# Softmax probabilities and values of a decoder's attention: from f32 to pairs of f16 halves

## What is computed

```python
def one_block(args):                       # 128 queries
    score = jnp.einsum('bqh,bqhs->bqs', iws, jax.nn.relu(dots))
    _, sel = lax.top_k(score, topk)        # 256 keys of each query
    kg, vg = gather_kv(sel)
    logits = jnp.einsum('bqgrd,bqkgd->bqgrk', qg, kg) * (HEAD_DIM ** -0.5)
    logits = jnp.where(valid, logits + bias, -jnp.inf)
    p = jax.nn.softmax(logits, axis=-1).astype(vg.dtype)
    o = jnp.einsum('bqgrk,bqkgd->bqgrd', p, vg)
```

## Time and profile before

| | |
|---|---|
| Median of 3 runs | 4112.12 us (4103.06 to 4114.4) |
| Profiled execution, its own time | 4099.31 us |
| Span of the profile | 4097.5 us |
| PE busy | 3281.3 us, 80% |
| DVE busy | 1911.3 us, 47% |
| ACT busy | 1566.2 us, 38% |
| POOL busy | 1078.0 us, 26% |
| Granted PE clock, mean | 0.90 |

### The profile page before, as it was taken

The page is one execution under the profiler, slowest core; times in us unless marked ns, Lnnn a source line. Parts: engine busy times, 40 slices in busy tenths (PEclk is TensorE's granted clock), DMA queues, the critical chain, the costliest instruction groups (busy, mean ns, idle before and its releaser), DMA issues.

```text
span 4097.5 us, 68214 instructions
## 1 busy us (share of the span) xinstructions
PE 3281.3 (80%) x26714; PEld 2622.8 (64%) x26714; DVE 1911.3 (47%) x3962; ACT 1566.2 (38%) x2674; POOL 1078.0 (26%) x979
## 2 busy tenths in 40 slices
PE   5958677288777897888798897889788897998597
PEld 3747555166455675677586785767667686676486
DVE  3635345634742235624474237732487324884100
ACT  2233332432632225432373226533265432754211
POOL 0131530022542114312341114311242112420142
PEclk9969888589889998899899999999999999999798
DMA  5426564045343453325252353414334043340254
GB/s 159 136 66 230 172 199 161 6 148 170 112 136 123 140 170 107 114 90 175 96 170 71 112 165 100 144 39 159 122 119 132 29 150 118 124 144 1 93 179 140
DMA packets 200579, 514.25 MB, mean 126 GB/s; under 512 B 20242, under 2 KB 79458, under 8 KB 200130
## 3 DMA queue, kind: packets, MB, share of 16 engines
q1 hardware_dynamic: 200258, 509.88, 38.1%
HBM read 443.67 MB, written 66.15 MB: 124 GB/s over the span
## 4 chain that ended last, share of the span: by engine, by line
issue 29%; PE 22%; ACT 8%; DVE 8%; POOLq 7%; POOL 4%; DMA 2%; ACTq 1%; DVEq 1%; SPq 0%
PE bank L784 4%; PE bank L785 4%; PE bank L786 4%; PE bank L833 4%; ACT T L1419 3%; DMA FR<-in_xT 2%; DVE T L1551 2%; POOLq L2016 1%; POOLq L2013 1%; POOLq L2011 1%; PE bank L822 1%; POOLq L1898 1%; POOL FR L2019 1%; ACTq L1421 1%; PE bank L809 1%
## 5 line engine op out<-in xcount | busy, mean ns | idle before, releaser
L784 PE MATMUL bank<-FR,ring 128*128 128x256 f16 (+1 forms) x4224 | 1189.3, 282 | 82.1 <-POOLq L580 23.7
L785 PE MATMUL bank<-FR,ring 128*128 128x256 f16 (+1 forms) x4224 | 1187.6, 281 | 0.0
L786 PE MATMUL bank<-FR,ring 128*128 128x256 f16 (+1 forms) x4224 | 1186.3, 281 | 0.0
L784 PEld LDWEIGHTS bank<-FR,ring 128*128 128x128 f16 x4224 | 423.0, 100 | 165.9 <-ACT ev L1360 27.4
L785 PEld LDWEIGHTS bank<-FR,ring 128*128 128x128 f16 x4224 | 420.6, 100 | 70.7 <-issue 1.1
L786 PEld LDWEIGHTS bank<-FR,ring 128*128 128x128 f16 x4224 | 420.3, 100 | 71.1
L784 PE MATMUL bank<-T,ring 128*128 128x256 f16 (+3 forms) x1280 | 370.2, 289 | 102.1 <-DVE kT L1661 52.4
L1551 DVE CUSTOM_DVE_ANT_0 T<-bank,T 128x256 f32<-128x256 f32 (+3 forms) x384 | 194.8, 534 | 531.8 <-PE bank L811 422.0
L833 PE MATMUL bank<-vtok,T 128*128 128x64 f32 x2176 | 321.2, 293 | 101.6 <-DVE T L1564 76.3
L833 PEld LDWEIGHTS bank<-vtok,T 128*128 128x128 f32 x2176 | 301.9, 213 | 126.8 <-issue 74.8
L785 PE MATMUL bank<-T,ring 128*128 128x256 f16 (+3 forms) x1280 | 369.1, 288 | 0.0
(11 more groups left out here) (305 smaller groups left out, 5970.4 us busy)
## 6 DMA issues: line engine op xcount, KB each, us to landing
ring<-halves_kept SPq DMA_DIRECT2D x605, 512.0 KB, 3.5
halves_kept<-ring SPq DMA_DIRECT2D x93, 512.0 KB, 5.2
ring<-halves_kept SPq DMA_DIRECT2D x52, 384.0 KB, 3.5
kT<-in_w_gu SPq DMA_DIRECT2D x33, 512.0 KB, 5.9
kT<-in_w_in SPq DMA_DIRECT2D x18, 512.0 KB, 5.9
ikT<-in_w_gu SPq DMA_DIRECT2D x17, 512.0 KB, 6.2
T<-in_xT SPq DMA_DIRECT2D x8, 1024.0 KB, 6.4
FR<-in_xT SPq DMA_DIRECT2D x8, 1024.0 KB, 10.0
```

The source lines that it names most:

```text
L784: mm(o, lhs[0], rhs[0], start=first, stop=False)
L785: mm(o, lhs[0], rhs[1], start=False, stop=False)
L786: return mm(o, lhs[1], rhs[0], start=False, stop=last)
```

## The change

Probabilities and values become pairs of f16 halves, scaled up by 1024 and 16 so that the low halves are not lost; `scale` divides by both. `values` is `three` f16 products (high x high, high x low, low x high) in place of one f32 product. ACT writes the high half of a group's probabilities (semaphore a_pTh); a new DVE instruction in `low_pT` reads the same bank again, multiplies and subtracts the high half, and only then counts a_pTc. DVE's order in step A of unit n is now: `mask` of n + 1, `low_pT` of group 0, `scale` of n - 2, `low_pT` of the other groups. The low half of the turned output is formed by DVE (`low_mix`) from PSUM, so that POOL's `mix_low`, ACT's second copy and the buffer mix32 go. The projection's values are written to an f32 buffer of their own (v32, for the output) and as the high half by ACT; DVE forms the low half. `PLAN` is the same.

```diff
-        vtok = sb("vtok", [128, SEQ // 128, 128])
+        vtok = sb("vtok", [128, SEQ // 128, 2, KVH * HD], F16)
+        v32 = sb("v32", [128, 2, KVH * HD])
-        pT = cut(T, 8192, 3, 4, 128)
+        pT = T[:, 8192:9728].bitcast(F16).rearrange("p (m s t n) -> p m s t n", s=2, t=4, n=128)
...
-                    last = mm(bank[6 + u % 2][:, 0:64], pT[:, GN[i, h, g] % 3, t % 4, :], vtok[:, t, e:e + 64],
-                              start=(t == 0), stop=(t == i))
+                    last = three(bank[6 + u % 2][:, 0:64], [pT[:, GN[i, h, g] % 3, s, t % 4, :] for s in range(2)],
+                                 [vtok[:, t, s, e:e + 64] for s in range(2)], t == 0, t == i)
...
-                A(pT[:, m % 3, 0:w, :], bank[4 + n % 2][:, 0:128 * w].rearrange("p (t n) -> p t n", n=128),
-                  ACT.Copy).then_inc(S("a_pTc"), 1)
+                A(pT[:, m % 3, 0, 0:w, :], bank[4 + n % 2][:, 0:128 * w].rearrange("p (t n) -> p t n", n=128),
+                  ACT.Copy, scale=P_UP).then_inc(S("a_pTh"), 1)
...
+                        A(v32[:, :, :], rows, ACT.Copy, scale=back)
+                        last = A(vtok[:, 2 * b:2 * b + 2, 0, :], rows, ACT.Copy, scale=V_UP * back)
...
+            def low_pT(i, h, g):
+                n, m = TN[i, h, g], GN[i, h, g]
+                dve.wait_ge(S("a_pTh"), n + 1)
+                w = min(4, i + 1 - 4 * g)
+                v.scalar_tensor_tensor(pT[:, m % 3, 1, 0:w, :],
+                                       bank[4 + n % 2][:, 0:128 * w].rearrange("p (t n) -> p t n", n=128), P_UP,
+                                       pT[:, m % 3, 0, 0:w, :], ALU.mult, ALU.subtract).then_inc(S("a_pTc"), 1)
+
+            def low_mix(i):
+                n = TN[i, "out", 0]
+                dve.wait_ge(S("a_pTh"), n + 1)
+                high, low = (mixA[:, s, :, 128 * (i % 2):128 * (i % 2) + 128] for s in range(2))
+                v.scalar_tensor_tensor(low, bank[4 + n % 2][:, :].rearrange("p (j n) -> p j n", n=128), M_UP, high,
+                                       ALU.mult, ALU.subtract).then_inc(S("a_pTc"), 1)
...
+                    if what == "v":
+                        wait_evacuated(dve, *step)
+                        v.scalar_tensor_tensor(vtok[:, 2 * b:2 * b + 2, 1, :], v32[:, :, :], V_UP,
+                                               vtok[:, 2 * b:2 * b + 2, 0, :], ALU.mult, ALU.subtract)
...
                 if kind == "A":
                     units = [(i, h) for i in tiles_of(b) for h in range(HEADS)]
                     n = step[2]
+                    i, h = units[n]
                     if n + 1 < UNITS:
                         mask(*units[n + 1])
+                    low_pT(i, h, 0)
                     if n >= 2:
                         scale(*units[n - 2])
+                    for g in range(1, groups(i)):
+                        low_pT(i, h, g)
+                    if n == HEADS + 1:
+                        low_mix(2 * b)
```

More of the change, by code:

```diff
@@ L56 @@
 I_UP = 16.0
+V_UP, P_UP = 16.0, 1024.0
 W_UP, H_UP, M_UP, U_UP = 256.0, 64.0, 16.0, 4.0
@@ L536, in layer @@
         relu = cut(T, 4096, 4, 512)
-        pT = cut(T, 8192, 3, 4, 128)
+        pT = T[:, 8192:9728].bitcast(F16).rearrange("p (m s t n) -> p m s t n", s=2, t=4, n=128)
         nearm = cut(T, 9728, 2, 256)
         osb = cut(T, 10240, 2, 512)
-        mix32 = cut(T, 11264, 4, 128)
         marks = T[:, 11776:12800].bitcast(F16)
@@ L562, in layer @@
         raw_room = [
-            vtok[:, 8:16, :].rearrange("p t n -> p (t n)").rearrange("p (a n) -> p a n", a=2),
+            vtok[:, 8:16, :, :].rearrange("p t s n -> p (t s n)").bitcast(F32).rearrange("p (a n) -> p a n", a=2),
             ikT[:, :, 1024:2048].bitcast(F32),
@@ L725, in _ @@
                     sp.dma_start(a["o_v"][t0:t0 + TOK].rearrange("(t p) n -> p t n", p=128),
-                                 vtok[:, 2 * b:2 * b + 2, :]).then_inc(S("outputs"), 16)
-                    outs += 16
+                                 v32[:, :, :]).then_inc(S("out_k"), 16)
                     if b == 0:
@@ L767, in _ @@
             sp.wait_ge(S("outputs"), outs)
-            sp.wait_ge(S("out_k"), 32 * NBLK)
+            sp.wait_ge(S("out_k"), 48 * NBLK)
             sp.wait_ge(S("out_gs"), 16)
@@ L1186, in copy_mix @@
                 act.wait_ge(S("a_pT"), n + 1)
[L1187 to L1191, removed]
+                A(mixA[:, 0, :, 128 * (i % 2):128 * (i % 2) + 128],
+                  bank[4 + n % 2][:, :].rearrange("p (j n) -> p j n", n=128), ACT.Copy, scale=M_UP
+                  ).then_inc(S("a_pTh"), 1)
             def sample_probs(s):
@@ L1251, in _ @@
                     if what == "v":
-                        last = A(vtok[:, 2 * b:2 * b + 2, :], o[:, 0:256].rearrange("p (t c) -> p t c", c=128), ACT.Copy,
-                                 scale=back)
+                        if b:
+                            act.wait_ge(S("out_k"), 48 * b)
+                        rows = o[:, 0:256].rearrange("p (t c) -> p t c", c=128)
+                        A(v32[:, :, :], rows, ACT.Copy, scale=back)
+                        last = A(vtok[:, 2 * b:2 * b + 2, 0, :], rows, ACT.Copy, scale=V_UP * back)
                         if b == 0:
@@ L1564, in scale @@
                 v.tensor_scalar(osb[:, i % 2, 64 * h:64 * h + 64], bank[6 + u % 2][:, 0:64],
-                                rden[:, u % 4:u % 4 + 1], None, ALU.mult).then_inc(S("a_scaled"), 1)
+                                rden[:, u % 4:u % 4 + 1], 1.0 / (P_UP * V_UP), ALU.mult, ALU.mult).then_inc(S("a_scaled"), 1)
             def biased(s):
@@ L1654, in _ @@
                             if b:
-                                dve.wait_ge(S("out_k"), 32 * b)
+                                dve.wait_ge(S("out_k"), 48 * b)
                             v.tensor_scalar(k32[:, j:j + nj, :], oj, back, None, ALU.mult)
@@ L1877, in _ @@
                     scale(2 * b + 1, HEADS - 1)
+                    low_mix(2 * b + 1)
         @block.gpsimd
@@ L1907, in near @@
                                 ).then_inc(S("a_near"), 1)
[L1909 to L1912, removed]
             for at, step in enumerate(PLAN):
@@ L2055, in _ @@
                         near(*units[n + 1])
[L2056 to L2059, removed]
 def outputs_of():
```

## The result

The changed kernel takes **4189.19 us** (median; 4186.02 to 4191.63), the kernel before 4113.26 us beside it (4103.06 to 4116.16): ratio 1.0186, 95% interval 1.0167 to 1.0205. It is 76 us slower. The spans of the two profiled executions differ by more, 4189.8 - 4097.5 = 92.3 us, because the one of before, at 4099.31 us, lies under all four of its timed runs and the one after, at 4191.63, is the slowest of its four. Differences between traces are held against 92.3 here, medians against 76.

A forecast was written before the change was run, and what follows sets the result against it. The bound was taken as a loop through three queues, not PE's busy time. Terms 21 + 51 - 8 + 3 (projection) + 18 gave +85 us: 4184 against the profiled 4099.3, written as 4193 for the median; range 4135 to 4245.

The forecast's parts named there:

- the parts: Exact-selection work at DVE's queue end in a block's early units: no longer hidden, stands behind the last low half; +51 us.
- the clock: PE's granted clock falls behind stops from bare selection work, in some 16 units at +1.2 each: +18 us.
- the gain at the turned output: POOL's `near` in the unit after the turned output no longer stands behind `mix_low`: 8 x -1, -8 us.
- PE: Values' products on PE: group of four tiles 0.35 us in place of 0.84, sparing PE 134 us over 1088 tiles.
- DVE: New low-half instruction on DVE: 0.69 us for 128x512, some 195 us in all, most of it in idle time.
- Ordinary units: Units' loop through three queues, by number of key groups, four to one: -3, +8, +13, +3, together +21 us.
- -3 for four groups: Four-group units, blocks 6 and 7: low halves eat PE's saving, -0.1 us a unit over 32 units, -3.
- the two signs: Prediction wrong if units with selection work keep their length, or plain units change by more than half a microsecond.
- The two-group term: Blocks 2 and 3: group 0's low half delays `scale` by about 0.9, less 0.49 on PE: +0.4 a unit, +13 us.
- three-group units: Blocks 4 and 5: one group behind exp takes 1.19 us where it took 0.95; +0.25 over 32 units, +8 us.
- rival 5: Lower PE clock spreads to ordinary late units: +60 us in place of +18, time 4235; chance 0.15.

The follow-up runs named there:

- exp_last_before: The kernel before, with ACT's exponential of the next unit moved behind all copies of this unit: 4098.81 us, ratio 0.998.
- late_and_exp_last: Changed kernel with `scale` before group 0's low half, PE's low-half pass one group later, ACT's next exponential behind all copies: 4050.05 us, ratio 0.9851.
- no_low_p: Changed kernel without the probabilities' low halves on DVE; the third pass takes the high half again, PE's work the same: 4011.32 us, ratio 0.9767.
- The pair without parts: Odd query tiles' exact selection on DVE left out of both kernels: changed kernel 4104.21 us (ratio 0.9981), kernel before 4097.53 us (0.9971).
- warm_block7: Changed kernel with useless PE products in block 7 alone, eight a unit and 20 to 40 behind each of its first four units: 4179.62 us, ratio 1.017.

## Why the prediction was right, and where it was off

The forecast was 4193 us, slower; the time is 4189. The mechanism is right where most of the loss is, in the units with parts. That the two numbers lie 4 us apart is in part luck: the sum of +85 stands against 76 measured, from a starting point of 4193 - 85 = 4108 where the kernel before took 4113. Its terms were too large for the parts and the clock and too large for the gain at the turned output, and these errors have opposite signs.

- **PE.** Right. A pass goes every 0.03 us at full clock, a group of four in 0.35 (3733.18 to 3733.54 in the timeline), every 0.05 at half (3730.82 to 3730.91). PE's busy time fell by 76 us and not by well over 100, because the granted clock fell too, 0.881 over the span; at equal clocks (0.894 in both `exp_last_before` and `late_and_exp_last`) it fell from 3286.9 to 3158.6, 128 us, and from 3281.3 to 3131.3, 150 us, between the kernel before (0.900) and `no_low_p` (0.902), against 134. The Trainium skill (TensorE: Matmul & The Clock Gate, Back-to-back issue gap) gives two figures: some 81 ns for sustained loads and products of 128 columns, and an isolated gap of N/2.4 + 2.5 ns. By that formula 64 columns would take 29 ns, an estimate. The trace agrees with the second, 0.35 us for twelve passes here and 0.055 for 128 columns in the earlier trace rows, although each of these passes has its own load.
- **DVE.** Right: 0.69 for 128x512 and 192.3 us in all, against 195.
- **The parts.** Right in mechanism, too large in size: 51 us, and 4.8 a block for the clock in blocks 4 to 7, some 70 together. Measured by block, 7 to 1, the clock included: 19.8, 13.4, 10.4, 8.3, 2.8, -2.4, 2.2, sum 54.5. The 15.5 + 4.8 said for block 7 is 20.3 against 19.8, but blocks 6, 5 and 4 had 15.6, 14.9 and 12.2 against 13.4, 10.4 and 8.3. The 3.0 us that the parts of block 7 were to show before are 1.1. The pair without parts gives 72 us by medians, 54 of it in these units, 10 in the others and the rest outside the intervals.
- **Ordinary units.** Predicted -3, +8, +13 and +3 for four groups to one; measured 7.2 (block 7's 7.3 of it is gone in `warm_block7`), 6.8, 2.9 and 0.4 (the table's second row, the units behind the turned output among them). So -3 for four groups, a plain unit unchanged at 8.8 in block 7, did not hold: they took 9.1 to 9.9, and the last ones 10.3 where they were 9.1. That is more than half a microsecond, one of the two signs that the prediction named for being wrong. What it had left out is the lower clock: at 1.00, in `warm_block7`, such units take 8.67, less than the 8.91 before, though group 0 waits for `scale` there too. The two-group term was too large: block 3's ordinary unit is 4.38 in place of 4.12, and many of those units lie under dense work. The three-group units are 6.67 in place of 6.53. Block 6's are unchanged at 7.65 when PE's clock is full, and take 8.6 where it is not. Granted clock of one such unit, then of two at full clock:

```profile
3259.90:3268.50 8.60, 0.16 (x1) 0.80 0.00 0
3276.30:3291.60 15.30, 0.31 (x2) 1.00 0.00 1
```

- **The turned output.** Wrong, if small. I took -8 us for `near` no longer standing behind `mix_low`. The eight units behind it differ by -2 in sum, and in block 6 the unit is longer, 9.98 where it was 8.92. The step that failed is that DVE's low half was taken to cost nothing in POOL's place. Block 6 after:

```profile
3297.82 0.60 ACT L1187 ACTIVATE mixA<-bank 128x512 f16<-128x512 f32 x1 [1.16 <-PE bank L842]
3298.45 0.69 DVE L1570 SCALAR_TENSOR_TENSOR mixA<-bank,mixA 128x512 f16<-128x512 f32 x1 [1.33 <-ACT mixA L1187]
3299.06 0.68 DVE L1552 CUSTOM_DVE_ANT_0 T<-bank,T 128x512 f32<-128x512 f32 x1
```

  The next `mask` (L1552) follows that low half with no idle time, 1.24 us behind the start of ACT's copy; before, it began 0.56 us behind it (3234.06 and 3233.50). What `near` behind `mix_low` had cost was a stop of 0.48 us later in the same mask.
- **The clock.** The place was wrong, and the size is open. I put 18 us behind the stops and nothing elsewhere. `warm_block7` gives back 2.3 behind the stops of block 7, where I had 4.8 and the clock rose only part of the way, and 7.3 in its ordinary units, where I had nothing, which is rival 5 in that block. The unit of block 6 above shows the same at 0.80, 8.6 for 7.65. What the clock costs in sum in blocks 4 to 6 was not tried.
- **The range.** What the sum didn't weigh is that its terms share one cause. The changed kernel without the low halves is at -99, the low halves in the loop +178. I had let these cancel unit by unit, which was right, but it hid that the order of four queues decides the sign.

## What to carry to other kernels

When an edit moves work from one engine to another, look at who waits for its new place and not at who is busy. The same 192 us of low halves cost 178 us inside the loop; once only a late pass waited for them the kernel was 0.4% faster than before, and with the exponential moved as well 1.5%, 55 us. And work at the tail of an engine's queue that was free may have been so only because nothing was late ahead of it: the selection parts went from 13 us to 85 without being touched.

## What of the hardware I had not expected

The granted clock fell in ordinary units too when PE's waits grew, from 8.2 us in five units to 13.6, with the longest going from 0.77 to 1.20: 0.87 over 47.8 us and 40.4 us, where the earlier trace rows have 1.00 with 8.9 us units, though no stop in them is as long as the 5.28 us at 3276.48 ahead of the slow clock of the earlier trace rows. Eight more products in each unit brought 1.00 and the old pace back. It happens without the selection parts as well (0.89). And it is not only the kernel's doing how long a stretch takes: between blocks 0 and 1 two programs that are equal there differed by 7.9 us in their profiled executions, so terms of a few microseconds can't be read from one pair of traces.
